# Shift and scale of the first modulation by column halves, and the input projection begun on two lower units

## The reference

```python
mod = jax.nn.silu(c) @ w_ada + b_ada                 # (1024) @ (1024, 6144)
sh1, sc1, g1, sh2, sc2, g2 = split(mod, 6)
h = rms_norm(x, norm1_g) * (1 + sc1) + sh1
proj = h @ w_in                                      # (256, 1024) @ (1024, 6400)
...
```

## Time and profile before

| | us |
|---|---|
| median of 3 runs | 1816.92 |
| the profiled execution, device time | 1816.28 |
| its span, first to last instruction | 1814.2 |
| PE busy in the span | 1778.0 (98%) |
| DVE busy | 1349.9 (74%) |
| ACT busy | 949.5 (52%) |

### The profile page before, as it was taken

One profiled execution on the slowest core, in us unless ns is written; L12 is line 12 of the kernel. 1 busy time (PEld: TensorE's weight loads), 2 busy tenths in 40 slices (PEclk: granted clock), 3 DMA queues, 4 the chain that ended last, 5 costly groups with the idle time before them and its releaser, 6 DMA issues.

```text
span 1814.2 us, 25435 instructions
## 1 busy us (share of the span) xinstructions
PE 1778.0 (98%) x9988; PEld 1519.4 (84%) x9988; DVE 1349.9 (74%) x1881; ACT 949.5 (52%) x1035; POOL 201.8 (11%) x173
## 2 busy tenths in 40 slices
PE   8999999999999999999999999999999999999998
PEld 3787757899999988888888888798979888888886
DVE  5679688589499966665666666758974779898897
ACT  2543574544454444444444444457644667667665
POOL 0000000388500024440000000000000000000000
PEclk9999999999999999999999999999999999999999
DMA  8655654555355568885555555554344688898894
GB/s 319 251 189 185 227 217 182 215 187 204 140 203 182 214 223 291 294 287 206 194 196 185 185 186 191 183 209 169 134 153 164 237 327 336 332 354 336 319 352 175
DMA packets 65552, 414.34 MB, mean 228 GB/s; under 512 B 8769, under 2 KB 9057, under 8 KB 19121
## 3 DMA queue, kind: packets, MB, share of 16 engines
q1 hardware_dynamic: 51904, 371.22, 55.6%
q0 software_dynamic: 7504, 25.80, 4.2%
q10 hardware_dynamic: 6050, 16.02, 2.2%
HBM read 395.45 MB, written 16.78 MB: 227 GB/s over the span
## 4 chain that ended last, share of the span: by engine, by line
PE 86%; DVE 7%; DMA 3%; ACT 2%; issue 1%; SPq 0%; DVEq 0%; ACTq 0%
PE ps L2442 23%; PE ps L2444 22%; PE ps L2443 22%; PE ps L2828 6%; PE ps L2857 3%; PE ps L2830 3%; DVE wlo L1320 2%; DMA BIG<-in_stream_dram 1%; ACT whi L758 1%; PE ps L3040 1%; DMA raw<-in_stream_dram 1%; DVE BIG L1405 1%; PE ps L2918 1%; DVE H L1359 1%; PE ps L2549 0%
## 5 line engine op out<-in xcount | busy, mean ns | idle before, releaser
L1320 DVE TENSOR_TENSOR wlo<-raw,whi 128x2048 fp32r<-128x2048 f32 x181 | 414.6, 2291 | 207.3 <-ACT whi L758 207.2
L758 ACT ACTIVATE whi<-raw 128x2048 fp32r<-128x2048 f32 x181 | 346.8, 1916 | 367.7 <-PE ps L2444 241.9
L2442 PE MATMUL ps<-whi,phi 128*128 128x512 f32 x608 | 237.7, 391 | 2.3 <-DVE plo L1927 2.3
L2443 PE MATMUL ps<-wlo,phi 128*128 128x512 f32 x608 | 236.6, 389 | 0.0
L2444 PE MATMUL ps<-whi,plo 128*128 128x512 f32 x608 | 236.6, 389 | 0.0
L2442 PE MATMUL ps<-whi,tboth 128*128 128x512 f32 (+1 forms) x576 | 226.5, 393 | 7.1 <-DVE wlo L1320 3.9
L2442 PE MATMUL ps<-tboth,whi 128*128 128x256 f32 x768 | 221.0, 288 | 2.9 <-DVE tboth L1342 2.8
L2444 PE MATMUL ps<-whi,tboth 128*128 128x512 f32 (+1 forms) x576 | 222.9, 387 | 0.0
L2443 PE MATMUL ps<-wlo,tboth 128*128 128x512 f32 (+1 forms) x576 | 222.6, 386 | 0.0
L2444 PE MATMUL ps<-tboth,wlo 128*128 128x256 f32 x768 | 217.2, 283 | 0.0
L2443 PE MATMUL ps<-tboth,whi 128*128 128x256 f32 x768 | 217.2, 283 | 0.0
(11 more groups left out here) (442 smaller groups left out, 3287.2 us busy)
## 6 DMA issues: line engine op xcount, KB each, us to landing
raw<-in_stream_dram SPq DMA_DIRECT2D x243, 1024.0 KB, 4.8
BIG<-in_stream_dram SPq DMA_DIRECT2D x90, 1024.0 KB, 6.6
BIG<-g_spill POOLq DMA_DIRECT2D x64, 128.0 KB, 4.7
s_spill<-MOD ACTq DMA_DIRECT2D x28, 256.0 KB, 2.0
late_units<-in_stream_dram SPq DMA_DIRECT2D x6, 1024.0 KB, 5.7
H<-in_stream_dram SPq DMA_DIRECT2D x6, 1024.0 KB, 4.8
BIG<-in_stream_dram SPq DMA_DIRECT2D x2, 2048.0 KB, 16.3
g_spill<-H ACTq DMA_DIRECT2D x4, 1024.0 KB, 5.4
```

The source lines that it names most:

```text
L758: nc.scalar.activation(hi_of(u), raw_of(u), ACT.Copy).then_inc(unit_hi, 1)
L1320: nc.vector.tensor_tensor(wlo[:, u % 2, :], raw_of(u), whi[:, u % 2, :].bitcast(f32), ALU.subtract).then_inc(unit_split, 1)
L2442: nc.tensor.matmul(out, ahi, bhi, start=start, stop=False)
L2443: nc.tensor.matmul(out, ahi, blo, start=False, stop=False)
```

## The change

Every load of units 0 to 7 is cut into two, column half 0 and column half 1 (each 0.5 MB, in runs of 512 elements). SP first loads half 0 of all eight units (`X` after unit 3), then W0, now into `MOD`, then half 1 of the units, with W2 after unit 3; W1 and W3 follow. PE does units 1, 3, 4 and 6 of half 0 and 1 and 3 of half 1, DVE the others. After half 0, DVE modulates columns 0 to 511, PE transposes groups 0 and 1 and does block 0 on W0 and, split, block 1 on W2; both upper units (W1, then W3) come after the transposes of groups 2 and 3. POOL's bias loads wait for `unit_used` 3.

```diff
+            first_sum(0, 0)
+            first_sum(0, 2)
+            norm(0, X, None)
+            first_sum(0, 5)
+            first_sum(0, 7, True)
+            first_modulated(0)
+            first_sum(1, 0)
+            first_sum(1, 2)
+            tr_low(T_H1, 0, (0, 1))
+            first_sum(1, 4)
+            first_sum(1, 5)
             lo(U_IN + 1)
...
+            first_sum(1, 6)
+            first_sum(1, 7, True)
+            first_modulated(1)
+            tr_low(T_H1, 0, (2, 3))
```

```diff
             for h in range(2):
+                for k, (first, last) in enumerate(ADA_LOADS):
+                    if h:
+                        sp.wait_ge(ada_loaded[k], 16 * (last - first))
+                    for c in range(first, last):
+                        sp.dma_start(both_halves(ada_raw[c], h),
...
+                    if last == 4 and h == 1:
+                        sp.dma_start(raw[:, 1, :], stream[DC + 2, :, :]).then_inc(raw_loaded[1], 16)
+                if h == 0:
+                    sp.dma_start(first_w, stream[DC, :, :]).then_inc(raw_loaded[0], 16)
             sp.wait_ge(raw_loaded[0], 16)
-            sp.dma_start(raw[:, 0, :], stream[DC + 2, :, :]).then_inc(raw_loaded[0], 16)
+            sp.dma_start(raw[:, 0, :], stream[DC + 1, :, :]).then_inc(raw_loaded[0], 16)
...
-            pool.wait_ge(unit_used, 2)
+            pool.wait_ge(unit_used, 3)
```

```diff
+            tr_high(T_H1, 0, (0, 1))
             hi(U_IN + 1, 0, in_at(1), 0)
-            for k in H1_ORDER:
...
+            tr_high(T_H1, 0, (2, 3))
             hi(U_IN + 2, 0, in_at(2), 0)
...
             transposes(T_H1, H, (0, 1))
             first_rows_part(0)
+            first_rows_part(1)
+            first_ada(1, ADA_BY_PE[1][1])
+            first_spread(1)
+            for t in range(TT):
+                pe.wait_ge(tr_lo, t + 1)
+                rows_part(2, U_IN + 1, 0, t, at=in_at(1))
             transposes(T_H1, H, (2, 3))
-            first_rows_part(1)
-            for t in range(TT):
-                pe.wait_ge(tr_lo, t + 1)
-                rows_part(0, U_IN, 1, t, at=in_at(0))
-            pe.wait_ge(tr_lo, 4)
-            block_rows(2, U_IN + 2, at=in_at(2))
+            for t in range(TT):
+                pe.wait_ge(tr_lo, 3 + t)
+                rows_part(0, U_IN + 1, 1, t, at=in_at(1))
+            for t in range(TT):
+                rows_part(2, U_IN + 2, 1, t, at=in_at(2))
```

More of the change, by code:

```diff
@@ L240, in hybrid_block_then_mixer_memory_moe_kernel, with ada_landed @@
         ada_in = {c: k for k, (first, last) in enumerate(ADA_LOADS) for c in range(first, last)}
-        ada_in_7 = len(ADA_LOADS)
+        def ada_landed(c, h):
+            first, last = ADA_LOADS[ada_in[c]]
+            return ada_loaded[ada_in[c]], 16 * (last - first) * (h + 1)
         def both_halves(rows, h):
             return rows.rearrange("p (k h n) -> p k h n", k=2, h=2)[:, :, h, :]
-        first_shift, first_scale = ([ps[:, 2 * h + k, :] for h in range(2)] for k in range(2))
+        first_shift, first_scale = ([ps[:, 6 * h + k, :] for h in range(2)] for k in range(2))
         first_rows = first_shift + first_scale
@@ L251, in hybrid_block_then_mixer_memory_moe_kernel @@
         ADA_PE = (0, 512, D)
-        first_w = ada_raw[0]
+        first_w = MOD[:, UW:2 * UW]
         ones = big[:, 16128:16128 + P]
@@ L419, in hybrid_block_then_mixer_memory_moe_kernel @@
         siluc_ready, ones_ready = sem("siluc_ready"), sem("ones_ready")
-        ada_loaded, ada_summed = [sem(f"ada_loaded{k}") for k in range(len(ADA_LOADS) + 2)], sem("ada_summed")
+        ada_loaded, ada_summed = [sem(f"ada_loaded{k}") for k in range(len(ADA_LOADS))], sem("ada_summed")
         b_ada_loaded, b_late_loaded = sem("b_ada_loaded"), sem("b_late_loaded")
@@ L512, in tr_bank @@
                 return 6 + k
+            if t == T_H1:
+                return 4 + k % 2
             return 4 + (k if t in HALVED or t in (T_OB, T_MEM) else (T_BASE[t] + k) % 2)
@@ L1416, in ada_out, with first_sum, first_modulated @@
                                                    ALU.add, ALU.add).then_inc(ada_free, 1)
[L1418 to L1440, removed]
+            def first_sum(h, c, ends=False):
+                dve.wait_ge(*ada_landed(c, h))
+                total, part = both_halves(ada_acc[0], h), both_halves(ada_raw[c], h)
+                if c == 0:
+                    last = nc.vector.tensor_scalar(total, part, siluc[:, c:c + 1], None, ALU.mult)
+                else:
+                    settle()
+                    last = nc.vector.scalar_tensor_tensor(total, part, siluc[:, c:c + 1], total, ALU.mult, ALU.add)
+                if ends:
+                    last.then_inc(ada_summed, 1)
+                else:
+                    mark(last)
+            def first_modulated(h):
                 dve.wait_ge(ada_full, h + 1)
@@ L2465, in transposes @@
                         pe.wait_ge(rows_ready, ROWS[t] - 2 * TT + k + 1)
+                        if t == T_H1 and k >= 2:
+                            pe.wait_ge(tr_lo, k - 1)
                     elif t == T_MEM:
@@ L2570, in _, with first_ada, first_spread @@
             pe.wait_ge(ones_ready, 2)
-            for c in ADA_BY_PE:
-                pe.wait_ge(ada_loaded[ada_in[c]], 16)
-                for m in range(4):
+            def first_ada(h, c):
+                pe.wait_ge(*ada_landed(c, h))
+                for m in (h, 2 + h):
                     nc.tensor.matmul(first_rows[m], silu_cols[:, c, :], ada_raw[c][:, m * 512:(m + 1) * 512],
                                      start=False, stop=False)
[L2577 to L2582, removed]
+            def first_spread(h):
+                pe.wait_ge(ada_summed, h + 1)
                 for m in (h, 2 + h):
@@ L2586, in _ @@
                 last.then_inc(ada_full, 1)
+            for c in ADA_BY_PE[0]:
+                first_ada(0, c)
+            first_spread(0)
+            first_ada(1, ADA_BY_PE[1][0])
             def first_rows_part(t):
```

39 lines of the change are left out of this document (11 added, 28 removed).

## The result

The changed kernel took 1823.78 us (median of 7 runs, 1822.02 to 1824.11), the kernel before beside it 1817.19 (7 runs, 1815.90 to 1818.71). The medians differ by 6.6 us; the ratio, which is not the quotient of the medians, is 1.0032 with a 95% interval of 1.0022 to 1.0041. The forecast of 1821.1 is 2.7 us low; the measured time is inside its range, close to the upper end, and slower by over 0.2% was its likeliest side. The profiled execution took 1823.83 with a span of 1821.7, 7.5 us longer than before's.

What follows compares the result with a forecast made beforehand. PE was taken to bound the kernel, so a later start moves the end by as much. W6 at 75.5 instead of 71.32 is +4.2 us, added to the median of 1816.92: 1821.1, with an 8-in-10 range of 1817.9 to 1824.2.

Steps and rivals of the forecast that it cites:

- The mechanism: Before PE's first product on W1: its split waits behind the copies of groups 2 and 3, 4.9 us lost.
- `ada_full` of half 0: End of half 0's sums on PE: forecast at 24.0 us, against 29.88 before.
- PE starts at 13.28 as before: First full-size matmuls: PE starts unchanged at 13.28, then 20 records take 10.7 us to the end of half 0.
- So I cost the cut at nothing: First loads: halves in runs of 512 elements load no slower than whole units, cost 0.
- the idle for DVE's sum: Half 1, before the sum is spread: PE waits from 35.9 to 37.3 for DVE, 1.4 us lost.
- The clock: Rival: PE's clock falls in the new idle before W1, W1 done at 58.2, time 1820.5 to 1823; chance 0.12.
- No idle in the rows here is as long as 4.9 us: Remark on the clock's fall in the idle before W1: the profile had no such idle, and 0.97 cost nothing.
- The rival's own consequence: After a clock fall the wait for W3 vanishes and POOL's loads start 1.8 us later than W5's; chance 0.12.
- All start together: Near 56.8 us: POOL's 3 MB of loads start with W5's load, which then takes 8.4 us, to 65.1.
- a collision at W5: W5's load beside POOL's lands at 65.1, putting W6 at 75.5; PE's own limit would give 72.8.
- the sum: The forecast's addition: W6 starts at 75.5 instead of 71.32, +4.2 us on the median, 1821.1.
- nothing later gives it back: After W6: the whole +4.2 us stays to the end, since PE never waits from 80 to 120 us.

Runs made afterwards that it cites:

- z1: y2 with the five small loads issued behind the first norm, at about 17 us, not at the start: 1815.09 us, 0.9987 of the kernel before.
- z2: The changed kernel in its own order, with only the loads of z1 (small loads and POOL's bias loads moved): 1825.71 us, 1.0043 of the kernel before.
- x4: The kernel before, in its old order, with only its eight first units loaded as two halves each: 1821.98 us, 1.0024 of the kernel before.
- x1: The changed kernel with 6 and 10 extra matmuls on constants in PE's two long idle times: 1827.23 us, 1.0049 of the kernel before.
- x3: The changed kernel with POOL's bias loads started at `unit_used` 2, not 3: 1833.47 us, 1.0085 of the kernel before.
- x2: The changed kernel with W1 split ahead of the copies of groups 2 and 3: 1825.28 us, 1.0038 of the kernel before.
- y1: x2 with DVE's last sums ahead of W2's `lo`, transposes between W2's token tiles, small loads at the start: 1820.71 us, 1.0024 of the kernel before.
- y2: y1 with POOL's two bias loads set apart and earlier, at `unit_used` 1 and 2: 1814.87 us, 0.9994 of the kernel before.
- y3: The kernel before with small loads at the start and bias loads at `h1_copied` 1 and `unit_used` 1: 1816.80 us, 1.0003 of the kernel before.

## Why the forecast was right, and where its terms were off

- **The mechanism held.** W1's split behind the transposes gave an idle of 4.96 us (4.9 forecast). z1 against z2 shows what the order costs, 8.0 us with equal loads.
- **`ada_full` of half 0 came at 23.9 (24.0 forecast) by luck.** "PE starts at 13.28 as before" failed: it started at 11.64, and then idled 1.26 us for DVE's sum, for which the forecast had no wait. The early start is an effect of the cut: in all nine kernels whose first units are halves PE's first work starts at 4.28 to 5.03, in the three with whole ones at 6.08 to 6.27.
- **"So I cost the cut at nothing" failed.** X landed at 14.0, not 12.1, and units 4 and 5 at 31.7, not 30.0; the text had priced each us there at a us. The argument took its rate from a queue that was full, and x4 shows the cost in an empty one. The Trainium skill's rule against DMAs under 1 MiB (DMA: Bandwidth & Descriptors, Measured (HBM→SBUF, 128 partitions, SWDGE, issued from GpSimd)) was rejected on that row; x4's rate from 2 to 4 us, 176 against 308 GB/s, agrees with it, and its nearly equal rate from 10 to 12 us, 408 against 428, doesn't. With units 4 and 5 late by 1.7 the idle for DVE's sum grew from 1.4 to 3.05, and with the low clock behind it W2 began at 41.97, not 39.1.
- **The clock, given 0.12, did fall, twice:** x1 measures 1.7 us in the sum and W2 and 2.5 in W1, together 4.2. The step that failed is "No idle in the rows here is as long as 4.9 us", from which a low chance was drawn: a row that shows 0.97 to be harmless says nothing of 3.05 or 4.96. The Trainium skill's warning against gaps (TensorE: Matmul & The Clock Gate, Why this matters for your kernels) agrees with this trace, 0.50 behind 3.05 and 4.96 us; behind x3's 3.08 and x4's 3.47 the clock stayed up. The rival's own consequence, no wait for W3, is what the trace shows.
- **W1 done at 62.4, not 56.1:** 1.9 from the late sum, 4.2 from the clock, and 0.2 that these two figures leave.
- **"All start together" failed.** With W1 that late, POOL's loads (62.80) began 4.1 us behind W5's (58.7, the end of W3's `lo`), so W5's was free and W6's took 8.47. Its cost at W6 was 1.07; PE's own pace from 62.4 gives 62.4 + 3 x 5.5 = 78.9, and with it 79.9. The forecast had charged 2.7 us (75.5 less 72.8) for a collision at W5. x2 has that collision, at 3.88, once W1 is early.
- **Why the time still came near:** the sum took too little for the start and the clock and too much for the loads: 72.8 + 6.3 + 1.07, less 0.3 of pace, is 79.9, where 75.5 was forecast. So W6 came 8.55 us late and not 4.2, twice as much. Of these 4.4 us 2.7 are left in the time: "nothing later gives it back" was off by 1.1, and the profiled execution of before lay 0.64 under the median to which the forecast added. That errors of both signs partly cancel is luck; direction and main cause are not.

What stays open: what the cut costs inside the changed kernel. x4 has it at 5.1 us in the old order, and z1, which keeps it, is no slower than before; no run has the new order with cheap halves. y1 and x1 lost 1 to 3 us more behind 200 us than their marks show, with the clock at 0.91 to 0.96 in some windows there, and y2 lost 1.4 between 1160 and 1268. One profile each doesn't say why. The mean granted clock goes with the time within one kernel too: z2's 1822.72 has 0.997, its 1828.91 has 0.994. Whether an order like z1's with small loads that disturb nothing would reach the 3 or 4 us that the head start promises wasn't tried.

## What to carry to other kernels

A head start on one engine is kept only if what it needs next is prepared ahead of the wait that it runs into. Here the split of W1 stood, in ACT's own order, behind copies that waited for PE itself. When a wait is taken out, look for the next limit before you count the gain (x1: 4.2 us freed, 1.5 left, then none): walk on until an engine is busy without a break. And price a small DMA at the place where it runs: at the head of an empty queue, or beside a bulk load, it isn't what it is in a full queue.

## What the runs showed of the hardware

- PE's granted clock went to 0.50 behind idle times of 2.64 (z2), 2.65 (z1), 3.05, 3.09 (x4), 3.37 (y1), 3.75 (x1), 3.88 (x2), 4.67 (x3) and 4.96 us, and to a mean of 0.58 over 20 to 22 us behind one of 2.13 (y1). It stayed behind 0.97, 1.26 and 2.40 (z2), and also behind 2.97 (x2, before W3), 3.08 (x3) and 3.47 (x4, at 24.75). So the length of one idle time doesn't tell whether the clock falls. The low stretch lasted 2 to 5 us. In x4's 3.09 and x2's 3.88 it came at the place where a load was late, so that a late load cost its wait and the slow restart.
- From 12 to 16 us of before the granted clock reads 1.00 while matmuls run at half pace, 0.86 us a record; there the pitch tells the level, and the clock column doesn't.
- A load of 1 MB takes 4.8 us to land over the whole run, 8.4 to 11.2 beside POOL's 3 MB. `positions`, 1 KB, takes 4.4 in the changed kernel, 8.1 in x4 and 12.53 behind them. The Trainium skill (DMA: Bandwidth & Descriptors, Queues, rings and completion order) says that each DMA engine takes turns between its queues; the doubled times beside POOL's queue agree with that, the 12.53 of 1 KB no row explains.
- The five small loads (273 KB) issued by ACT delayed the bulk loads beside them by 1.5 to 3.5 us wherever they stood: X by 1.5 (y3), 2.3 (y2) and 3.5 (y1), PE's unit 1 of half 1 by 2.4 (26.52 in z1, 24.14 in the changed kernel).
